# Half of a causal depthwise convolution moved from VectorE to GpSimd, inside a fused two-model forward pass

## The chip, the cores and the metric

The kernel is one program on one core of a Trainium2 chip. The core has five engines with an instruction queue each: TensorE (PE in the profile, its weight loads PEld), VectorE (DVE), ScalarE (ACT), GpSimd (POOL) and SyncE (SP, which here only issues transfers). They meet through semaphores alone. The metric is the device time of one execution, in microseconds, as the median of several runs.

## The reference

The program computes two models one behind the other on 256 tokens of width 1024: first a model of two layers (an "even" and an "odd" one), then a second of two layers with a feed-forward block, a mixer and another feed-forward block each. The change lies in the even layer of the first. Its left half is a gated convolution over time, 512 channels wide:

```
def _conformer_conv(u_val, u_gate, w_dw, b_dw, ln_g, ln_b):
    c = u_val.shape[-1]
    h = u_val * jax.nn.sigmoid(u_gate)
    h = jnp.pad(h, ((0, 0), (CONV_WIDTH - 1, 0), (0, 0)))
    y = lax.conv_general_dilated(h, w_dw[:, None, :].astype(h.dtype), (1,), 'VALID',
                                 dimension_numbers=('NWC', 'WIO', 'NWC'), feature_group_count=c)
    y = _layernorm(y + b_dw.astype(y.dtype), ln_g, ln_b)
    return jax.nn.silu(y)
```

The convolution is depthwise: each channel is the sum of 31 taps (CONV_WIDTH), a shifted copy of its own row times one weight. Its right half is causal attention with 8 heads of 64. Both halves are gated and go through one output projection, whose result is added to x.

## The kernel before

**Layout.** Activations lie channels on partitions, tokens along the row. The 512 channels of the convolution are four tiles of 128 channels by 256 tokens: `conv[:, c, :]`, with c from 0 to 3, and `hpad[:, c, :]`, the gated input with 30 zeros ahead of it. So tap k of tile c reads `hpad[:, c, k:k + 256]`, multiplies it by one weight per partition and adds it to `conv[:, c, :]`.

**The jobs.** The even layer projects its input in 14 jobs on TensorE (`job`, matmuls at line 697). Each takes two or four weight tiles in float32 as three passes of a high and a low part. ScalarE makes the high part of a weight tile (line 1346) and VectorE the low one (line 1727, `split_to`); the job waits for `tile_lo`. There is room for 6 split tiles (RING), so a tile's high part waits for the job that read its place last. ScalarE brings each job's result from PSUM.

**The convolution.** After job 3 VectorE multiplies value by gate into `hpad` (line 1808) and starts the four sums with tap 0 and the bias (line 1811). The other 30 taps are single instructions, a product and an addition in one (line 1818), put by hand in between: `taps(a, b)` is a loop over taps a to b - 1, four channel tiles each. Two taps (8 instructions) come behind the splits for each of jobs 4 to 12, which makes taps 1 to 18. Two more come in each of six hooks in the attention, taps 19 to 30.

**The attention.** It runs four pairs of heads in a pipeline of steps s = 0, 1, ... In one step VectorE takes the scores of pair s out of PSUM (line 1771), forms the negated maxima (lines 1774 and 1775), runs the hook, and scales the exponentials of pair s - 1 by their reciprocal sums (lines 1788, 1789, 1794; semaphore `p_made`). Three steps later it gates the pair's output (line 1839). ScalarE takes the exponentials (line 1395), TensorE turns them (line 797), ScalarE copies them out (line 1403), and TensorE multiplies by the values (line 772). Scores are made at line 760.

**What follows.** The output projection (line 811) takes the attention's half of the channels first. Ahead of its first matmul (`y_wait`, k == 4) TensorE waits for all taps and sums the four tiles of `conv` over the channels (line 838), which the layer norm needs. VectorE centres the tiles (line 1841), ScalarE squares them, TensorE sums the squares (line 843), and VectorE scales and gates (lines 1844 and 1846) while the projection of the attention's half runs.

**GpSimd** has four memsets and four transfers at the start (lines 640 to 650), and then three transfers that wait for far later layers (lines 658 and 660). It computes nothing else. `sg` is a scratch tile, unused in the even layer.

Of the kernel before, what the change touches and what calls it, by code (L numbers as in the profile page):

```python
# [17 lines left out]
ALU = mybir.AluOpType  # L18
# [6 lines left out]
T = 256  # L25
# [7 lines left out]
CONV = 31  # L33
# [325 lines left out]
def build(nc, x_in, stream, params, csts, bias_in, lora_in, final_g, vb2, sinks, out):  # L359
    ctx = ExitStack()  # L360
    with ctx:
        def sb(name, *shape):
            return ctx.enter_context(nc.sbuf_tensor(name, [P, *shape], F32))

        def flat(ap):
            return ap.rearrange("p a b -> p (a b)")
# [3 lines left out]
        def sem(name):  # L370
            if name not in names:
                names[name] = ctx.enter_context(nc.semaphore(name))
            return names[name]
# [9 lines left out]
        sg = sb("silu_gate", SS, T)  # L383
# [6 lines left out]
        def par(name, lo=0, n=None):  # L390
            o, w = PAR.at[name]
            return PARt[:, o + lo:o + (w if n is None else lo + n)]

        def cst(name, lo=0, n=None):
            o, w = CST.at[name]
            return CSTt[:, o + lo:o + (w if n is None else lo + n)]
# [20 lines left out]
        def at(*shape):  # L417

            n = int(np.prod(shape))
            o = place[0]  # L420
            place[0] = o + n
            assert o + n <= ARENA, o + n
            a = arena[:, o:o + n]
            if len(shape) == 1:
                return a
            letters = "abcdef"[:len(shape)]
            return a.rearrange(f"p ({' '.join(letters)}) -> p {' '.join(letters)}",
                               **{c: s for c, s in zip(letters, shape)})
# [38 lines left out]
        hpad = at(4, CONV - 1 + T + 2)  # L467
        ugate = at(4, T)
        conv = at(4, T)
# [163 lines left out]
        def arena_free(n):  # L633


            return n - 1 if n and PHASES[n - 1][0].startswith("ffn") else n

        @block.gpsimd
        def _(pool):
            pool.memset(hpad[:, :, 0:CONV - 1], 0.0)  # L640
            pool.memset(hidv.rearrange("p a b c d -> p (a b c d)"), 0.0)
            pool.memset(VCB.rearrange("p a b c -> p (a b c)"), 0.0)
            pool.memset(SC.rearrange("p a b c d -> p (a b c d)"), 0.0).then_inc(sem("zeros_made"), 1)

            pool.wait_ge(sem("x_loaded"), 16 * NTT)
            pool.wait_ge(sem(f"w_loaded{NS - 1}"), 16)
            pool.dma_start(CSTt[:, CST_HEAD:], csts[:, CST_HEAD:]).then_inc(sem("const_loaded"), 16)
            pool.dma_start(DIST.rearrange("p a b c -> p (a b c)"), bias_in).then_inc(sem("const_loaded"), 16)
            pool.dma_start(SINK, sinks.broadcast_to([P, NH])).then_inc(sem("const_loaded"), 16)
            pool.dma_start(VB2, vb2.broadcast_to([P, HD])).then_inc(sem("const_loaded"), 16)  # L650
            for l in range(2):

                n = [i for i, p in enumerate(PHASES) if p[:2] == ("mix", l)]
                if n:
                    pool.wait_ge(sem("const_loaded"), CONSTS)
                    if arena_free(n[0]):
                        pool.wait_ge(sem("x_made"), 4 * arena_free(n[0]))
                    pool.dma_start(lora[:], lora_in[l]).then_inc(sem("lora_loaded"), 16)
            pool.wait_ge(sem("x_made"), 4 * arena_free(len(PHASES)))
            pool.dma_start(FG, final_g.broadcast_to([P, D])).then_inc(sem("gain_loaded"), 16)  # L660
# [3 lines left out]
        def _(pe):  # L664
# [75 lines left out]
            def headnorm(kind, hn0, i, bank):  # L740

                width = HEADNORMS[kind][i][1]
                pe.wait_ge(sem("sq_made"), hn0 + i + 1)
                pe.matmul(PS[:, bank, 0:width], cst("blk"), sq[:, i, 0:width], start=True, stop=True)\
                  .then_inc(sem("ssq_made"), 1)
# [74 lines left out]
            def even_layer(tr0, jb0, hn0, n):  # L820
                for i in range(10):
                    job("even", tr0, jb0, i)
                for i in range(4):
                    headnorm("even", hn0, i, 4 + i)
                for i in range(10, 14):
                    job("even", tr0, jb0, i)
                pe.wait_ge(sem("job_out"), jb0 + 14)

                pe.wait_ge(sem("qk_made"), 4)
                attention("even", {"q": Q1}, {"k": lambda j, rows: K1[rows, j, :]}, lambda s: None)  # L830

                def y_wait(k):


                    if k == 4:
                        pe.wait_ge(sem("conv_step"), 4 * CONV)
                        for c in range(4):
                            ins = pe.matmul(PS[:, 4, 0:T], cst("ones"), conv[:, c, :], start=(c == 0), stop=(c == 3))
                        ins.then_inc(sem("ln_sum_made"), 1)
                    if k == 6:  # L840
                        pe.wait_ge(sem("convsq_made"), 1)
                        for c in range(4):
                            ins = pe.matmul(PS[:, 4, T:2 * T], cst("ones"), convsq[:, c, :],
                                            start=(c == 0), stop=(c == 3))
                        ins.then_inc(sem("ln_sum_made"), 1)
                    if k == 0:
                        pe.wait_ge(sem("y_conv_made"), 1)
                pe.wait_ge(sem("pair_out"), 4)
                out_projection("even", tr0, n, y_wait)
# [832 lines left out]
        def _(dve):  # L1682
            dve.wait_ge(sem("head_loaded"), HEAD)
            dve.wait_ge(sem("zeros_made"), 1)
            done = Steps(dve, "dve_step")
            for gain in ("b_q", "c_q", "d_q"):
                k = done(dve.tensor_scalar(par(gain), par(gain), HD ** -0.5, None, ALU.mult))
# [43 lines left out]
            def split_for(n):  # L1731

                split_to(SPLIT[now["kind"]][2][n])
# [70 lines left out]
            def even_layer(jb0, hn0):  # L1804
                for n in range(4):
                    split_for(n)
                dve.wait_ge(sem("job_out"), jb0 + 4)
                done.wait(done(dve.tensor_tensor(hpad[:, :, CONV - 1:CONV - 1 + T], conv, ugate, ALU.mult)))
                o = PAR.at["conv_w"][0]
                for c in range(4):  # L1810
                    dve.tensor_scalar(conv[:, c, :], hpad[:, c, 0:T], par("conv_w", c, 1), par("conv_b", c, 1),
                                      ALU.mult, ALU.add).then_inc(sem("conv_step"), 1)

                def taps(a, b):
                    with dve.Fori(a, b) as k:
                        for c in range(4):
                            dve.wait_ge(sem("conv_step"), k * 4 + (c - 3))
                            dve.scalar_tensor_tensor(conv[:, c, :], hpad[:, c, bass.ds(k, T)],  # L1818
                                                     PARt[:, bass.ds(k * 4 + (o + c), 1)], conv[:, c, :],
                                                     ALU.mult, ALU.add).then_inc(sem("conv_step"), 1)  # L1820

                for n in range(4, 14):
                    split_for(n)
                    for i in {11: [0], 12: [1], 13: [2, 3]}.get(n, []):
                        a, gain = ((Q1, "b_q"), (K1, "b_k"))[i // 2]
                        j = 2 * (i % 2)
                        scaled(hn0, i, [(flat(a[:, j:j + 2, :]), gain)])
                    if n < 13:  # L1830
                        taps(2 * n - 7, 2 * n - 5)

                def hook(s):
                    if s < 6:
                        taps(2 * s + 19, 2 * s + 21)

                dve.wait_ge(sem("job_out"), jb0 + 14)
                dve.wait_ge(sem("const_loaded"), CONSTS)
                attention("even", lambda c, pv: dve.tensor_tensor(YT[:, c.tile, :], pv, ZB[:, c.j, :], ALU.mult), hook)
                dve.wait_ge(sem("ln_sum_made"), 1)  # L1840
                dve.scalar_tensor_tensor(conv, rep(PS[:, 4, 0:T], 4), -1.0 / 512, conv, ALU.mult, ALU.add)\
                   .then_inc(sem("conv_centred"), 1)
                dve.wait_ge(sem("lnrs_made"), 1)
                dve.tensor_tensor(conv, conv, rep(lnrs, 4), ALU.mult).then_inc(sem("conv_scaled"), 1)
                dve.wait_ge(sem("conv_act"), 1)
                dve.tensor_tensor(YT[:, 0:4, :], conv, ZA, ALU.mult).then_inc(sem("y_conv_made"), 1)
# [345 lines left out]
```

## Time and profile before

| | |
|---|---|
| median of 3 runs | 1607.51 us |
| lowest and highest | 1598.91 and 1611.56 us |
| the profiled execution, its time | 1599.55 us |
| its span, first to last instruction | 1597.8 us |
| mean granted TensorE clock in it | 0.955 |
| busy: TensorE, VectorE, ScalarE, GpSimd | 91%, 54%, 43%, 0% |
| even layer, from the span's start | about 172 us |

All rows are from the one profiled execution. In a row of the timeline the first number is the start in us from the span's start, the second the us to the end of the group; then come engine, line, operation, the tile written and the tile read, shapes and count; idle time ahead of it stands in brackets with what ended it. The convolution's tiles lie in a large buffer which the profile calls `arena`. An instruction's duration includes its way in and out of the engine, and the next one starts a little before it ends: what a row of equal instructions costs is the distance from the first start to the next group's start.

### The profile page before, as it was taken

How to read it: one execution, taken by the hardware profiler on the slowest of the kernel's cores; microseconds unless marked ns; L12 is line 12 of the kernel's file. 1: busy time of each engine (PE TensorE's matmuls, PEld its weight loads, DVE VectorE, ACT ScalarE, POOL GpSimd, SP SyncE). 2: the span in 40 equal slices, each digit the busy share in tenths (PEclk: the TensorE clock that was granted, in tenths of full speed). 3: DMA queues.
4: the chain of work that ended last, by engine and by line, in shares of the span. 5: the costliest groups of instructions: out<-in, count | busy, mean ns of one | idle time of the engine just before them, and what ended most of it. 6: DMA issues, size and time to landing. Idle time of an engine off the chain costs nothing.

```text
span 1597.8 us, 28298 instructions
## 1 busy us (share of the span) xinstructions
PE 1455.9 (91%) x11842; PEld 1273.8 (80%) x11842; DVE 858.4 (54%) x1226; ACT 692.9 (43%) x1048; POOL 5.9 (0%) x15
## 2 busy tenths in 40 slices
PE   6977886888999989888899998999989988899998
PEld 6964676755899989767499998999989867489997
DVE  5876416744545557634454555545566644364554
ACT  5443336543444456421344444444445422254443
POOL 1000000000000000000000000000000000000000
PEclk9986998899999999979999998999999979999999
DMA  7421444115455444200455543555534200445552
GB/s 291 184 80 39 159 148 168 41 40 196 173 197 184 175 154 158 80 2 3 158 202 192 190 170 130 205 185 197 176 140 167 110 1 3 152 178 197 182 178 100
DMA packets 21741, 227.10 MB, mean 142 GB/s; under 512 B 2449, under 2 KB 2449, under 8 KB 3617
## 3 DMA queue, kind: packets, MB, share of 16 engines
q1 hardware_dynamic: 20880, 221.30, 37.9%
q0 software_dynamic: 784, 4.70, 0.9%
q8 instruction: 59, 0.97, 0.2%
q14 instruction: 18, 0.14, 0.0%
HBM read 224.94 MB, written 1.05 MB: 141 GB/s over the span
## 4 chain that ended last, share of the span: by engine, by line
PE 77%; DVE 11%; ACT 7%; DMA 3%; issue 2%; DVEq 0%; SPq 0%; ACTq 0%; PEldq 0%
PE PS L697 46%; PE PS L1005 14%; PE PS L811 6%; DMA weight_ring<-in_stream 2%; DVE w_lo L1945 2%; DVE w_lo L1727 1%; ACT arena L1323 1%; DVE arena L1703 1%; PE PS L1127 1%; PE PS L1185 1%; PE PS L1160 1%; ACT w_hi L1346 1%; PE PS L1191 1%; DVE arena L1818 1%; PE PS L1122 1%
## 5 line engine op out<-in xcount | busy, mean ns | idle before, releaser
L697 PE MATMUL PS<-hT_hi,w_hi 128*128 128x256 f32 x2136 | 615.1, 288 | 39.9 <-DVE hT_lo L1709 22.1
L697 PE MATMUL PS<-hT_lo,w_hi 128*128 128x256 f32 x2136 | 610.9, 286 | 0.0
L697 PE MATMUL PS<-hT_hi,w_lo 128*128 128x256 f32 x2136 | 610.9, 286 | 0.0
L697 PEld LDWEIGHTS PS<-hT_hi,w_hi 128*128 128x128 f32 x2136 | 416.6, 195 | 50.1 <-issue 46.1
L697 PEld LDWEIGHTS PS<-hT_lo,w_hi 128*128 128x128 f32 x2136 | 416.7, 195 | 3.8 <-issue 0.7
L697 PEld LDWEIGHTS PS<-hT_hi,w_lo 128*128 128x128 f32 x2136 | 416.4, 195 | 0.0
L1945 DVE TENSOR_TENSOR w_lo<-weight_ring,w_hi 128x1024 fp32r<-128x1024 f32 x176 | 207.2, 1219 | 17.7 <-ACT w_hi L1522 17.7
L1951 DVE TENSOR_TENSOR w_lo<-weight_ring,w_hi 128x1024 fp32r<-128x1024 f32 x88 | 107.8, 1225 | 156.6 <-ACT w_hi L1528 156.6
L1522 ACT ACTIVATE w_hi<-weight_ring 128x1024 fp32r<-128x1024 f32 x176 | 175.4, 1046 | 19.6 <-DMA weight_ring<-in_stream 19.6
L1727 DVE TENSOR_TENSOR w_lo<-weight_ring,w_hi 128x1024 fp32r<-128x1024 f32 x107 | 125.7, 1220 | 62.9 <-ACT w_hi L1346 62.7
L1528 ACT ACTIVATE w_hi<-weight_ring 128x1024 fp32r<-128x1024 f32 x88 | 93.1, 1058 | 104.4 <-PE PS L1005 104.4
L1005 PE MATMUL PS<-w_hi,act_hi 128*128 128x512 f32 x352 | 138.0, 392 | 0.0
L1005 PE MATMUL PS<-w_hi,act_lo 128*128 128x512 f32 x352 | 138.0, 392 | 0.0
L1005 PE MATMUL PS<-w_lo,act_hi 128*128 128x512 f32 x352 | 136.9, 389 | 0.0
L1548 ACT ACTIVATE silu_gate<-PS 128x256 f32<-128x256 f32 x88 | 33.7, 383 | 233.8 <-PE PS L697 233.8
L1346 ACT ACTIVATE w_hi<-weight_ring 128x1024 fp32r<-128x1024 f32 x107 | 106.5, 1050 | 28.4 <-DMA weight_ring<-in_stream 28.4
L1964 DVE TENSOR_TENSOR ffn_act<-silu_gate,PS 128x256 f32<-128x256 f32 x88 | 37.1, 421 | 144.5 <-ACT silu_gate L1548 144.5
L811 PE MATMUL PS<-weight_ring,yT 128*128 128x512 f32 x256 | 111.5, 594 | 0.6 <-issue 0.6
L811 PEld LDWEIGHTS PS<-weight_ring,yT 128*128 128x128 f32 x256 | 48.9, 191 | 61.4 <-issue 61.1
L1005 PEld LDWEIGHTS PS<-w_lo,act_hi 128*128 128x128 f32 x352 | 66.1, 188 | 14.4
L1005 PEld LDWEIGHTS PS<-w_hi,act_hi 128*128 128x128 f32 x352 | 66.4, 189 | 11.5
L1005 PEld LDWEIGHTS PS<-w_hi,act_lo 128*128 128x128 f32 x352 | 66.4, 189 | 10.6
(277 smaller groups left out, 1370.5 us busy)
## 6 DMA issues: line engine op xcount, KB each, us to landing
weight_ring<-in_stream SPq DMA_DIRECT2D x139, 1536.0 KB, 6.6
consts<-in_csts POOLq DMA_DIRECT2D x1, 1864.0 KB, 7.8
arena<-in_bias_in POOLq DMA_DIRECT2D x1, 1152.0 KB, 9.6
x_res<-in_x_in SPq DMA_DIRECT2D x2, 512.0 KB, 4.2
lora<-in_lora_in POOLq DMA_DIRECT2D x2, 512.0 KB, 5.4
x_out<-yT SPq DMA_DIRECT2D x2, 512.0 KB, 2.6
arena<-in_final_g POOLq DMA_DIRECT2D x1, 512.0 KB, 7.0
params<-in_params SPq DMA_DIRECT2D x1, 292.5 KB, 5.4
```

The costliest lines, as they stand in the source:

```text
L697: ins = pe.matmul(out, w[a], x[b], start=(start and i == 0), stop=(stop and i == 2))
L811: ins = pe.matmul(PS[:, 2 * t + half, :], YT[:, k, t * P:(t + 1) * P], w[:, half * 512:(half + 1) * 512], start=(i == 0), stop=(i == 7))
L1005: ins = pe.matmul(o, (Ah, Al)[x][:, s, t * P:(t + 1) * P], w[y][:, cols], start=(start and j == 0), stop=(stop and j == 2))
L1122: pe.matmul(o, Vret[:, c2, (2 * e + j) * P:(2 * e + j + 1) * P], STm[:, e, j, c2, :], start=True, stop=False)
L1346: act.activation(Wh[:, q % RING], Wr[:, tile % (3 * NS)], ACT.Copy).then_inc(sem("tile_hi"), 1)
L1522: act.activation(Wh[:, 3 * (i % SS) + part], Wr[:, 3 * (g % NS) + part], ACT.Copy)\
L1528: act.activation(Wh[:, 3 * (i % SS) + 2], Wr[:, 3 * ((tr0 + i) % NS) + 2], ACT.Copy)\
L1548: act.activation(sg[:, s, :], PS[:, 4 + s, 0:T], ACT.Silu).then_inc(sem("silu_made"), 1)
L1727: dve.tensor_tensor(Wl[:, q % RING], Wr[:, tile % (3 * NS)], Wh[:, q % RING], ALU.subtract)\
L1945: dve.tensor_tensor(Wl[:, u], Wr[:, 3 * ((tr0 + i) % NS) + part], Wh[:, u], ALU.subtract)\
L1951: dve.tensor_tensor(Wl[:, u], Wr[:, 3 * ((tr0 + i) % NS) + 2], Wh[:, u], ALU.subtract)\
L1964: dve.tensor_tensor(aT[:, s, :], sg[:, s, :], PS[:, 4 + s, T:2 * T], ALU.mult)\
```

## The change

Channel tiles 2 and 3 are computed on GpSimd. It waits for `conv_gated`, which VectorE now raises behind the gating product. Then, tap by tap, it does a product into the scratch tile `sg` and an addition into `conv`, each waiting for what it reads. VectorE keeps tiles 0 and 1, two instructions for a tap. It now takes three taps behind each of jobs 4 to 12 (taps 1 to 27, six instructions where eight stood) and one tap in each of the first three hooks (taps 28 to 30, two instructions where eight stood); hooks 3 to 5 are empty. TensorE's wait ahead of the channel sum becomes two: `conv_step` for VectorE's tiles and `conv_tap` for GpSimd's. VectorE waits for `conv_tap` as well ahead of the centring.

```
+            pool.wait_ge(sem("conv_gated"), 1)
+            for k in range(CONV):
+                for c in (2, 3):
+                    if k == 0:
+                        pool.tensor_scalar(conv[:, c, :], hpad[:, c, 0:T], par("conv_w", c, 1), par("conv_b", c, 1),
+                                           ALU.mult, ALU.add).then_inc(sem("conv_tap"), 1)
+                    else:
+                        pool.wait_ge(sem("conv_tap"), 2 * (k - 1) + (c - 2) + 1)
+                        pool.tensor_scalar(sg[:, c - 2, :], hpad[:, c, k:k + T], par("conv_w", 4 * k + c, 1), None,
+                                           ALU.mult).then_inc(sem("conv_part"), 1)
+                        pool.wait_ge(sem("conv_part"), 2 * (k - 1) + (c - 2) + 1)
+                        pool.tensor_tensor(conv[:, c, :], conv[:, c, :], sg[:, c - 2, :], ALU.add)\
+                            .then_inc(sem("conv_tap"), 1)
...
-                        pe.wait_ge(sem("conv_step"), 4 * CONV)
+                        pe.wait_ge(sem("conv_step"), 2 * CONV)
+                        pe.wait_ge(sem("conv_tap"), 2 * CONV)
...
-                done.wait(done(dve.tensor_tensor(hpad[:, :, CONV - 1:CONV - 1 + T], conv, ugate, ALU.mult)))
+                dve.tensor_tensor(hpad[:, :, CONV - 1:CONV - 1 + T], conv, ugate, ALU.mult).then_inc(sem("conv_gated"), 1)
+                dve.wait_ge(sem("conv_gated"), 1)
...
-                        for c in range(4):
-                            dve.wait_ge(sem("conv_step"), k * 4 + (c - 3))
+                        for c in range(2):
+                            dve.wait_ge(sem("conv_step"), k * 2 + (c - 1))
...
-                        taps(2 * n - 7, 2 * n - 5)
+                        taps(3 * n - 11, 3 * n - 8)
...
-                    if s < 6:
-                        taps(2 * s + 19, 2 * s + 21)
+                    if s < 3:
+                        taps(s + 28, s + 29)
...
+                dve.wait_ge(sem("conv_tap"), 2 * CONV)
```

## Rows read from the trace of the kernel before

**Rows 1.** The page: busy time by engine, and the chain's shares by line.

```profile
PE 1455.9 (91%) x11842; PEld 1273.8 (80%) x11842; DVE 858.4 (54%) x1226; ACT 692.9 (43%) x1048; POOL 5.9 (0%) x15
PE PS L697 46%; PE PS L1005 14%; PE PS L811 6%; DMA weight_ring<-in_stream 2%; DVE w_lo L1945 2%; DVE w_lo L1727 1%; ACT arena L1323 1%; DVE arena L1703 1%; PE PS L1127 1%; PE PS L1185 1%; PE PS L1160 1%; ACT w_hi L1346 1%; PE PS L1191 1%; DVE arena L1818 1%; PE PS L1122 1%
```

**Rows 2.** Busy time by stretch: jobs 4 to 13, attention, start of the output projection.

```profile
core 0: us, PE busy (x) PEld busy (x) DVE busy (x) ACT busy (x) POOL busy (x), PEclk, DMA share, GB/s
45.70:77.10 31.40, 31.40 (x263) 31.40 (x262) 30.61 (x59) 12.52 (x17) 0.00 (x0) 1.00 0.46 169
77.10:105.10 28.00, 26.68 (x200) 24.39 (x199) 18.96 (x34) 15.59 (x20) 0.00 (x0) 1.00 0.31 113
105.10:140.70 35.60, 17.36 (x89) 10.53 (x88) 33.33 (x81) 12.33 (x38) 0.00 (x0) 0.58 0.00 1
140.70:151.80 11.10, 11.06 (x25) 6.24 (x26) 1.23 (x1) 1.06 (x1) 0.00 (x0) 0.80 0.00 0
```

**Rows 3.** What TensorE waited for, 0 to 185 us: us, times, longest.

```profile
PE PS L797 <- DVE arena L1794: 9.1, 4, 3.9
...
PE PS L697 <- DVE w_lo L1727: 1.3, 1, 1.3
```

**Rows 4.** Timeline of VectorE: gating product, splits, and first taps.

```profile
43.20 1.23 DVE L1808 TENSOR_TENSOR arena<-arena 128x1024 f32<-128x1024 f32 x1 [2.33 <-ACT arena L1410]
...
45.77 2.35 DVE L1727 TENSOR_TENSOR w_lo<-weight_ring,w_hi 128x1024 fp32r<-128x1024 f32 x2
48.03 3.25 DVE L1818 SCALAR_TENSOR_TENSOR arena<-arena,params 128x256 f32<-128x256 f32 x8
```

**Rows 5.** Groups of VectorE, 45.7 to 105.2: busy us, mean ns, idle before.

```profile
L1818 DVE SCALAR_TENSOR_TENSOR arena<-arena,params 128x256 f32<-128x256 f32 x72 | 29.2, 478 | 0.0
L1727 DVE TENSOR_TENSOR w_lo<-weight_ring,w_hi 128x1024 fp32r<-128x1024 f32 x16 | 18.9, 1220 | 9.8 <-ACT w_hi L1346 9.8
L1758 DVE SCALAR_TENSOR_TENSOR arena<-arena,params 128x512 f32<-128x512 f32 x4 | 2.9, 744 | 0.0
```

**Rows 6.** Timeline of VectorE in the attention: parts of steps 2 to 5.

```profile
120.29 3.25 DVE L1818 SCALAR_TENSOR_TENSOR arena<-arena,params 128x256 f32<-128x256 f32 x8
123.45 0.16 DVE L1788 TENSOR_SCALAR arena<-arena 128x4 f32<-128x4 f32 x1
123.65 0.18 DVE L1789 RECIPROCAL arena<-arena 128x4 f32<-128x4 f32 x1
123.86 1.03 DVE L1794 TENSOR_TENSOR arena<-arena 128x256 f32<-128x256 f32 x2
124.81 0.95 DVE L1771 SCALAR_TENSOR_TENSOR arena<-arena,PS 128x768 f32<-128x768 f32 x1
...
130.29 1.03 DVE L1794 TENSOR_TENSOR arena<-arena 128x256 f32<-128x256 f32 x2
...
136.43 3.25 DVE L1818 SCALAR_TENSOR_TENSOR arena<-arena,params 128x256 f32<-128x256 f32 x8
```

**Rows 7.** The chain that ended last, end of the attention: start, us, what.

```profile
136.23 1.55 PE PS L797 x6
137.81 0.82 ACT lora L1403
138.67 1.57 PE PS L772 x8
140.26 0.43 DVE yT L1839
140.74 3.78 PE PS L838 x8
```

**Rows 8.** Timeline of GpSimd: two of its memsets.

```profile
0.74 0.20 POOL L640 MEMSET arena<- 128x120 f32 x1 [0.29 <-POOLq L2181]
0.88 0.53 POOL L641 MEMSET arena<- 128x512 f32 x1
1.34 0.53 POOL L642 MEMSET arena<- 128x512 f32 x1
```

More of the change, by code:

```diff
@@ L1815, in taps @@
                     with dve.Fori(a, b) as k:
-                        for c in range(4):
-                            dve.wait_ge(sem("conv_step"), k * 4 + (c - 3))
+                        for c in range(2):
+                            dve.wait_ge(sem("conv_step"), k * 2 + (c - 1))
                             dve.scalar_tensor_tensor(conv[:, c, :], hpad[:, c, bass.ds(k, T)],
```

## The prediction

> **What bounds the kernel now.** I read the page first: TensorE is busy 91% of the span, and the taps of line 1818 are 1% of the chain that ended last [rows 1]. So the change can only matter in the even layer's 172 us, and I read that layer stretch by stretch. In the jobs, from 45.7 to 105.1 us, TensorE hardly ever stands still and VectorE is busy too, 30.61 of the first 31.40 us [rows 2]; all the same TensorE waited for a split only once, 1.3 us [rows 3]. In the attention it is the other way round: VectorE is busy 33.33 of 35.60 us and TensorE 17.36 [rows 2], and TensorE's longest wait in all is for VectorE's scaling, 9.1 us [rows 3]. The attention is VectorE's stretch, and taps are a large part of it. It ends with a chain through TensorE, ScalarE and VectorE; at 140.74 TensorE begins the channel sum, which needs every tap [rows 7]. That is the point at which I measure both paths of the changed kernel.
>
> **What the change removes.** One tap on one tile costs VectorE 0.395 us: eight of them take from 120.29 to 123.45 [rows 6]. In the jobs 72 become 54 [rows 5], which frees 18 x 0.395 = 7.1 us. TensorE doesn't wait there, so this is worth nothing by itself, but it is slack, and I need it below. In the attention each of six hooks takes 3.16 us [rows 6]. Hook 5, at 136.43, runs beside the last chain [rows 6, 7] and is already free. Hooks 0 to 4 lie in VectorE's row: 5 x 3.16 = 15.8 us go, and 6 instructions of 0.395 stay in hooks 0 to 2, 2.4 us. That is 13.4 us gross. Not all of it is had. With the hooks gone the last two pairs run nose to tail on TensorE and ScalarE. From the end of pair 2's scaling, 130.29 + 1.03 = 131.3, to the end of the last gating product, 140.7, there are now 9.4 us. The work of two pairs in a row is 2 x (1.55 + 0.82 + 1.57) + 0.43 = 8.3 us [rows 7]. So the hook in this piece is worth 1.1 and not 3.2, and 2.1 us are given back. Net 11.3: without GpSimd's half the sum could begin at 140.7 - 11.3 = 129.4 us.
>
> **What it adds.** GpSimd waits for the gating product, which ends at 43.20 + 1.23 = 44.4 [rows 4]; its transfers are long issued. Then it does 2 first products and 60 pairs of a product and an addition, in order, the addition waiting for the product just before it. Nothing else is queued behind them but transfers for much later layers. TensorE's new wait is the costly one. The channel sum, the whole output projection, and behind them the residual and the next layer stand behind it in TensorE's queue. VectorE and ScalarE have nothing else to do by then, so each us by which GpSimd is late costs one us. Break even is at (140.7 - 44.4 - 0.6) / 60 = 1.59 us a pair; the whole gain is there below (129.4 - 45.0) / 60 = 1.41 us.
>
> No row shows a product or an addition on GpSimd. The nearest are its memsets. One of 512 columns costs 1.34 - 0.88 = 0.46 us, one of 120 costs 0.14 [rows 8], so about 0.25 us for 256 columns. That is one pass over a tile. Lower end: both instructions cost like memsets, 0.50 us a pair. Upper end: a product is two passes (a read, a write) and an addition three, none of them overlapped and each as dear as the 512-column memset, 5 x 0.46 = 2.3 us. I take five passes at the half of that, for half the columns: 5 x 0.23 = 1.15 us. To this come semaphores. On VectorE two tiny instructions that wait for each other start 0.20 us apart [rows 6]; one such wait in a pair, and a little for the other, is 0.25 us. So 1.40 us a pair if GpSimd is alone: it would end at 45.0 + 84 = 129, at the very moment when the attention does.
>
> The Trainium skill's page "GPSIMD Engine Reference", Performance versus the Vector engine, measures an addition of 2048 float32 columns at 4497 ns on GpSimd. An eighth of it is an estimate of 0.56 us for ours, beside 0.69 by my passes; by that the pair would be 1.27 us and the end 121. No row of before shows such an addition.
>
> It isn't alone. VectorE runs two-input instructions on the same memory nearly all the time: splits at (48.03 - 45.77) / 2 = 1.13 us [rows 4], 16 of them; 54 taps at 0.395; 4 instructions of line 1758 at about 0.67, their mean of 744 ns less the 0.08 by which a tap's 478 ns is over its 0.395 [rows 5]; in the attention 6 taps and 8 scalings at about 0.475 [rows 6]. This is 18.1 + 21.3 + 2.7 + 2.4 + 3.8 = 48.3 us, or 0.80 us for each pair of GpSimd. The disturbance to GpSimd lies between nothing and all of that: a pair costs 1.40 to 2.20 us. No row has the two engines at work together, so I take a little under the middle, 0.35 us, since GpSimd has the end of the attention, and the 9.8 us in which VectorE waits [rows 5], to itself. Then a pair is 1.75 us and GpSimd ends at 45.0 + 105 = 150.0. The channel sum begins at 150 in place of 140.7: **+9.3 us**. The attention at 129.4 is covered by it; its gain goes into a wait.
>
> **The clock.** The granted clock is 0.58 over the attention and 0.80 in the stretch behind it [rows 2]. The channel sum already starts at the lower level of 1.2 GHz after a thin stretch. So a longer wait changes nothing at this place, and I add nothing.
>
> **Sum.** The profiled execution took 1599.55 us (span 1597.8, and 1.75 around it); with +9.3 it is 1608.9. The median of the runs shown is 8.0 us above that execution, and I carry this over: 1607.5 + 9.3 = 1617.
>
> **Rivals.**
> 1. *GpSimd is in time.* A pair costs 1.41 us or less, also beside VectorE; the attention sets the end. For it: my price for GpSimd alone is just that, and much of the memset's price may be overlapped reading and writing. Against it: VectorE's two-input work. Result: 129.4 in place of 140.7, -11.3 us, 1596. Even this is only 0.7%.
> 2. *The two engines hold each other up, and the jobs starve* (the other side). If each two-input instruction of VectorE waits for one instruction of GpSimd, 1.15 / 2 = 0.575 us, the 74 of them in the jobs add 42.5 us and only 7.1 are slack, so the jobs end 35.4 us later. The 14 in the attention add 8. By then GpSimd is done or nearly so, and the channel sum starts at 129.4 + 35.4 + 8 = 173: +32 us, 1640. With x us for each instruction the sum moves by 74x - 7.1 + 14x - 11.3, which is over 16 us from x = 0.39. For it: VectorE is busy 30.61 of 31.40 us in the jobs [rows 2]. Against it: GpSimd's own gaps let VectorE through. The Trainium skill states this as a rule, in "SBUF — State Buffer", Who interferes with whom: a VectorE instruction with two SBUF inputs and a GpSimd one that reads SBUF share a read interface, the first to start holds it for its whole length, and the other is blocked. No row of before has both at work, so none agrees or disagrees yet.
> 3. *GpSimd's instructions are simply dear.* At the upper end of 2.3 us and 0.25 for semaphores a pair costs 2.55 us; the end is at 45 + 153 = 198, +57 us, 1665. For it: memsets are the simplest thing that the engine does. Against it: nothing that the profile shows.
>
> **Chances.** A measurement of this kernel tells about 1% from no change, 16 us. My forecast, GpSimd last with a pair at 1.6 to 1.85 us (0 to +16): 0.45. Rival 1 (down to -11, with run scatter perhaps -16): 0.20. Rival 2: 0.20, of which a third stays under +16. Rival 3, from +16 to +57: 0.15. Faster by over 1% is then 0.05, mostly scatter on rival 1; within 1% is 0.43 of the forecast, 0.15 of rival 1 and some of rival 2, rounded to 0.60; slower 0.35. The range goes from rival 1 with a little scatter, 1594, to well into rivals 2 and 3, 1650. The likeliest case alone is 1607 to 1624.
>
> **What would show it.** GpSimd's rows: pair after pair from 44.5 us, spaced 1.75 us, and closer together while VectorE waits around 80 us and from 130 us on. VectorE's taps in the jobs start-to-start at about 0.4 us, and jobs that end near 105: right for me; 0.6 us and more, with TensorE waiting for line 1727, is rival 2. The last gating product (line 1839) near 130. Ahead of TensorE's channel sum an idle time of 20 us that GpSimd ended: if it is missing, rival 1; if it is 60 us, rival 3. I am wrong in kind if anything outside the even layer moves.

## The result

The changed kernel takes 1630.11 us, the median of 4 runs from 1628.53 to 1631.39. The kernel before takes 1604.97 us (4 runs, 1598.91 to 1611.56). The ratio is 1.0159, with a 95% interval of 1.0125 to 1.0193: slower by 1.6%, about 25 us. I had forecast 1617 us and no difference that can be told from none. The change cost nearly three times the 9.3 us of my sum.

The profiled execution took 1631.39 us with a span of 1629.6, against 1599.55 and 1597.8: 31.8 us of span. That is more than the 25.1 us between the medians, because the profiled execution of the kernel before lies 5.4 us under its median and that of the changed kernel 1.3 over. The page of the changed kernel shows GpSimd in the chain that ended last, with 4% and 3% of the span for its two lines; in the kernel before it wasn't there at all [rows 1].

```profile
PE 1457.4 (89%) x11842; PEld 1274.5 (78%) x11842; DVE 852.7 (52%) x1164; ACT 692.8 (43%) x1048; POOL 125.6 (8%) x137
PE 73%; DVE 9%; POOL 7%; ACT 6%; DMA 3%; issue 2%; SPq 0%; DVEq 0%; ACTq 0%; PEldq 0%
PE PS L710 41%; PE PS L1019 14%; PE PS L824 6%; POOL silu_gate L659 4%; POOL arena L662 3%; DMA weight_ring<-in_stream 2%; DVE w_lo L1961 2%; DVE w_lo L1741 1%; ACT arena L1337 1%; DVE arena L1717 1%; PE PS L1141 1%; PE PS L1199 1%; PE PS L1205 1%; PE PS L1136 1%; ACT w_hi L1360 1%
```

Two queries place the loss. First, what TensorE waited for in the first 215 us (us, times, longest); then its timeline at that wait. Line 852 is the channel sum, line 662 GpSimd's addition.

```profile
PE PS L852 <- POOL arena L662: 33.6, 1, 33.6
...
PE PS L710 <- DVE w_lo L1741: 3.1, 2, 1.8
```

```profile
134.84 1.55 PE L785 MATMUL PS<-lora,arena 128*64 128x256 f32 x8 [0.90 <-ACT lora L1417]
169.98 3.55 PE L852 MATMUL PS<-arena,consts 128*128 128x256 f32 x8 [33.60 <-POOL arena L662]
```

The attention is over, TensorE does its last product with the values at 134.84, and then it stands still for 33.6 us until GpSimd's last addition. The channel sum starts at 169.98 in place of 140.74 [rows 7], 29.2 us later. At the first addition of the layer's output to x the two kernels are at 200.19 and 171.56 us, 28.6 apart, and at the same place of the odd layer 28.1. The other 3.7 us of the 31.8 come up in the later layers, which do the same in both. The four executions of the kernel before lie 12.7 us apart, so I read nothing into them.

The stretches of [rows 2] in the changed kernel, in the same columns: GpSimd is busy throughout, VectorE has 25.13 us of work in the third where it had 33.33, and in the fourth nothing but GpSimd moves.

```profile
45.70:77.10 31.40, 30.12 (x252) 29.94 (x251) 31.40 (x41) 12.56 (x18) 30.48 (x25) 1.00 0.46 166
...
105.10:140.70 35.60, 21.43 (x123) 14.55 (x122) 25.13 (x46) 12.34 (x38) 34.01 (x39) 0.64 0.00 0
140.70:151.80 11.10, 0.00 (x0) 0.00 (x0) 0.00 (x0) 0.00 (x0) 10.60 (x14) 0.50 0.00 0
```

GpSimd's own groups over the whole span: count, busy us, mean ns of one, idle before.

```profile
L659 POOL TENSOR_SCALAR silu_gate<-arena,params 128x256 f32<-128x256 f32 x60 | 71.2, 1187 | 0.0
L662 POOL TENSOR_TENSOR arena<-arena,silu_gate 128x256 f32<-128x256 f32 x60 | 46.3, 771 | 5.0
L655 POOL TENSOR_SCALAR arena<-arena,params 128x256 f32<-128x256 f32 x2 | 3.4, 1680 | 27.5 <-DVE arena L1822 27.5
```

Its timeline shows two prices for the same pair. Beside VectorE's splits a product takes up to 2.95 us. With VectorE quiet, a pair takes (168.11 - 132.27) / 21 = 1.71 us: product to addition 1.00, addition to product 0.70.

```profile
45.23 3.35 POOL L655 TENSOR_SCALAR arena<-arena,params 128x256 f32<-128x256 f32 x2 [27.47 <-DVE arena L1822]
48.57 1.08 POOL L659 TENSOR_SCALAR silu_gate<-arena,params 128x256 f32<-128x256 f32 x1
...
97.01 2.94 POOL L659 TENSOR_SCALAR silu_gate<-arena,params 128x256 f32<-128x256 f32 x1
100.04 1.00 POOL L662 TENSOR_TENSOR arena<-arena,silu_gate 128x256 f32<-128x256 f32 x1
...
132.27 0.92 POOL L659 TENSOR_SCALAR silu_gate<-arena,params 128x256 f32<-128x256 f32 x1
133.28 0.72 POOL L662 TENSOR_TENSOR arena<-arena,silu_gate 128x256 f32<-128x256 f32 x1
133.98 0.92 POOL L659 TENSOR_SCALAR silu_gate<-arena,params 128x256 f32<-128x256 f32 x1
...
168.11 0.92 POOL L659 TENSOR_SCALAR silu_gate<-arena,params 128x256 f32<-128x256 f32 x1
```

And VectorE pays as well. These are its groups from 45.7 to 105.2 us, answering to [rows 5], and a stretch of its timeline, where six taps go from 54.51 to 58.23: 0.62 us each, where eight took 3.16 [rows 6]. A split's mean is 1387 ns where it was 1220.

```profile
L1833 DVE SCALAR_TENSOR_TENSOR arena<-arena,params 128x256 f32<-128x256 f32 x49 | 31.3, 703 | 0.0
L1741 DVE TENSOR_TENSOR w_lo<-weight_ring,w_hi 128x1024 fp32r<-128x1024 f32 x16 | 21.5, 1387 | 6.1 <-ACT w_hi L1360 6.1
```

```profile
54.51 3.80 DVE L1833 SCALAR_TENSOR_TENSOR arena<-arena,params 128x256 f32<-128x256 f32 x6
58.23 2.55 DVE L1741 TENSOR_TENSOR w_lo<-weight_ring,w_hi 128x1024 fp32r<-128x1024 f32 x2
```

A quarter fewer taps thus took more time. In this window 49 of the 54 keep VectorE busy for 31.3 us, where all 72 took 29.2, and the last matmul of the jobs starts at 109.01 us instead of 104.82. That loss of 4.2 us lies under GpSimd's late end and isn't seen in the time. It becomes visible as soon as GpSimd is made faster, as the first experiment shows.

### The profile page after: what moved, and what is told of

The parts are those of the page before. It is cut to its first block, busy times and chain, and to the rows that moved or that the text cites. A ratio compares the mean times of both kernels' runs of the same rounds, so it can differ in the third digit from the quotient of the medians.

```text
span 1629.6 us, 28256 instructions
## 1 busy us (share of the span) xinstructions
PE 1457.4 (89%) x11842; PEld 1274.5 (78%) x11842; DVE 852.7 (52%) x1164; ACT 692.8 (43%) x1048; POOL 125.6 (8%) x137
## 3 DMA queue, kind: packets, MB, share of 16 engines
HBM read 224.94 MB, written 1.05 MB: 139 GB/s over the span
## 4 chain that ended last, share of the span: by engine, by line
PE 73%; DVE 9%; POOL 7%; ACT 6%; DMA 3%; issue 2%; SPq 0%; DVEq 0%; ACTq 0%; PEldq 0%
PE PS L710 41%; PE PS L1019 14%; PE PS L824 6%; POOL silu_gate L659 4%; POOL arena L662 3%; DMA weight_ring<-in_stream 2%; DVE w_lo L1961 2%; DVE w_lo L1741 1%; ACT arena L1337 1%; DVE arena L1717 1%; PE PS L1141 1%; PE PS L1199 1%; PE PS L1205 1%; PE PS L1136 1%; ACT w_hi L1360 1%
```

## The experiments

My theory after the result: GpSimd's chain is last by its own price, 1.71 us a pair and not 1.40, and it and VectorE hold each other up. The rival: the price is ordinary, and the mutual blocking makes both dear. The 1.71 us in the stretch where VectorE is quiet already speak against it as a whole. Beside these stands the question whether the loss in the jobs is real when GpSimd is not last.

Edits are shown against the changed kernel, except in the last two experiments: the first of these starts from the kernel before, the second from the first. A ratio is to the kernel before, measured again each time: 1606.58 us for the first experiment and for the taps placed otherwise, 1602.35 us for the one tile and for GpSimd in the attention only. A time without a ratio is of a single execution, good for its trace and not for a difference of a few us.

**The product as a tensor_tensor.**

```
-                        pool.tensor_scalar(sg[:, c - 2, :], hpad[:, c, k:k + T], par("conv_w", 4 * k + c, 1), None,
-                                           ALU.mult).then_inc(sem("conv_part"), 1)
+                        pool.tensor_tensor(sg[:, c - 2, :], hpad[:, c, k:k + T],
+                                           par("conv_w", 4 * k + c, 1).broadcast_to([P, T]), ALU.mult)\
+                            .then_inc(sem("conv_part"), 1)
```

> The changed kernel, but each product on GpSimd is a tensor_tensor with the weight broadcast along the row, in place of a tensor_scalar that takes the weight as a scalar operand. In the changed kernel the product costs 1.00 us from start to start and the addition 0.70 us, once VectorE is quiet. Theory A (the dear thing is the tensor_scalar with its scalar operand): the product falls to 0.8 us or less, a pair to about 1.5 us, the channel sum starts about 12 us earlier than 169.9 us, the kernel takes 1618 us. Theory B (any multiplying instruction costs that, or reading hpad does): the product stays at 1.00 us and the kernel at 1630 us. If two tensor inputs were what costs, as my passes had it, it would become slower.

Measured: 1614.82 us, ratio to before 1.0058 (1.0033 to 1.0082). Theory A holds for the price; the channel sum starts at 154.75 us, 15.2 earlier than in the changed kernel. With VectorE quiet the product now takes 0.69 us from start to start, like the addition, and a pair 1.37 us:

```profile
151.14 0.72 POOL L663 TENSOR_TENSOR arena<-arena,silu_gate 128x256 f32<-128x256 f32 x1
151.82 0.61 POOL L659 TENSOR_TENSOR silu_gate<-arena,params 128x256 f32<-128x256 f32 x1
152.51 0.72 POOL L663 TENSOR_TENSOR arena<-arena,silu_gate 128x256 f32<-128x256 f32 x1
```

The product went from 1.00 to 0.69 us although it now reads a second tensor. So it was the form of the instruction that was dear, not the passes over memory. But look at VectorE in the same run, and at TensorE's waits:

```profile
55.06 5.00 DVE L1834 SCALAR_TENSOR_TENSOR arena<-arena,params 128x256 f32<-128x256 f32 x6
59.97 3.32 DVE L1742 TENSOR_TENSOR w_lo<-weight_ring,w_hi 128x1024 fp32r<-128x1024 f32 x2
```

```profile
PE PS L711 <- DVE w_lo L1742: 8.1, 2, 6.3
PE PS L774 <- DVE arena L1773: 7.9, 1, 7.9
PE PS L811 <- DVE arena L1809: 5.5, 3, 3.1
...
PE PS L853 <- POOL arena L663: 5.0, 1, 5.0
```

Six taps take 4.91 us, 0.82 each, over twice the 0.395 of before. GpSimd's instructions start 0.76 to 0.88 us apart at this place, so the two engines take turns, one tap to one instruction. TensorE waits 8.1 us for splits, and 7.9 ahead of the attention's first scores, which wait for line 1773: these start at 121.56 us, where they started at 105.79 before the change and at 110.47 in the changed kernel. The attention ends at 150 us, almost 10 later than before the change, and GpSimd still ends 5 us behind it. So the faster GpSimd delays VectorE more: of the 33.6 us that TensorE waited for it, 15.2 are gained, and only 5 are left because the attention itself now ends 13 us later. This is the mechanism of my rival 2.

**GpSimd only writes.**

```
-            for k in range(CONV):
...
+            for k in range(180):
+                if k:
+                    pool.wait_ge(sem("conv_tap"), k)
+                pool.memset(sg[:, :, :].rearrange("p a b -> p (a b)"), 0.0).then_inc(sem("conv_tap"), 1)
```

> Leaves out the two channel tiles of GpSimd: it writes zeros to the scratch tile 180 times instead, each waiting for the one before, and reads nothing. VectorE's work is that of the changed kernel. If what slows VectorE's taps from 0.395 to about 0.63 us and its splits is GpSimd's reading, taps go back to 0.395 us, the jobs end near 105 us and the attention near 129.4 us. If any work of GpSimd on the memory slows VectorE, taps stay at 0.5 us or more and the jobs end near 109. GpSimd's writes end at 45 + 180 x 0.5 to 0.6 = 135 to 153 us, so the attention's end must be read in the trace and the time is set by those writes: 1595 to 1615 us.

Measured: 1607.21 us, a single execution. VectorE's two-input instructions go as if GpSimd weren't there, though that engine is busy 28.3 of the 31.4 us from 45.7 us on. Groups from 45.7 to 105.2:

```profile
L1825 DVE SCALAR_TENSOR_TENSOR arena<-arena,params 128x256 f32<-128x256 f32 x54 | 22.9, 481 | 0.2 <-DVE arena L1825 0.2
L1733 DVE TENSOR_TENSOR w_lo<-weight_ring,w_hi 128x1024 fp32r<-128x1024 f32 x16 | 18.9, 1220 | 14.5 <-ACT w_hi L1352 14.5
```

The means are 481 and 1220 ns, against 478 and 1220 in [rows 5], and VectorE waits 14.5 us for ScalarE where it waited 9.8. The last matmul of the jobs starts at 104.29 us. So GpSimd's writing costs the taps and splits nothing; what holds them up goes away with its reading. (The run leaves out the arithmetic together with the reads and doesn't part the two.)

One form is held up even by writes: VectorE's tensor_scalar, which has one tensor as input. The small one on 4 columns (line 1788 before, 1794 here) lasts 163 ns in the mean before and 407 here, up to 560. The reciprocal just behind it stays at 178 ns. The two first products of VectorE's tiles, also tensor_scalars, take 1.23 us here, where four took 1.30 before. In the changed kernel the small one lasts 377 ns in the mean.

The run also shows the floor of the attention: its last gating product (line 1846) starts at 126.73.

```profile
122.15 0.56 DVE L1794 TENSOR_SCALAR arena<-arena 128x4 f32<-128x4 f32 x1 [0.74 <-ACT arena L1401]
...
126.73 0.42 DVE L1846 TENSOR_TENSOR yT<-PS,arena 128x256 f32<-128x256 f32 x1 [2.08 <-PE PS L777]
```

It ends at 127.2 us, where the prediction had 129.4 for an undisturbed VectorE. The Trainium skill states this in "SBUF — State Buffer", Who interferes with whom: a VectorE instruction with two SBUF inputs shares a read interface with a GpSimd one that reads SBUF, and doesn't meet one that only writes. By that rule the traces agree, 0.62 and 0.82 us a tap beside reads and 0.41 beside writes.

**VectorE without its taps.**

```
-                        pe.wait_ge(sem("conv_step"), 2 * CONV)
+                        pe.wait_ge(sem("conv_step"), 2)
...
-                        taps(3 * n - 11, 3 * n - 8)
...
-                        taps(s + 28, s + 29)
```

> Leaves out taps 1 to 30 of VectorE's two channel tiles; GpSimd's work is that of the changed kernel. In the changed kernel its 60 pairs took 121.3 us, 2.02 a pair, and 1.71 once VectorE was quiet. If the 0.31 us between is VectorE's two-input instructions holding it up, and more of that is taps than splits, a pair falls to about 1.80 us, GpSimd ends near 49 + 108 = 157 us and the kernel takes about 1617 us. If GpSimd runs at 2.02 whatever VectorE does, it ends at 170 and the time stays at 1630. The jobs end at 105 to 106 us.

Measured: 1624.16 us, a single execution. GpSimd's pairs run from 48.57 to 166.8 us, 1.97 us each, where they took 2.02. I had expected 1.80. The taps thus cost GpSimd only 0.05 us a pair; of the 0.31 between a quiet and a mean pair nearly all is left when they are gone. The trace shows what does it. Both engines at one place, VectorE's splits first:

```profile
56.85 2.70 DVE L1741 TENSOR_TENSOR w_lo<-weight_ring,w_hi 128x1024 fp32r<-128x1024 f32 x2 [2.86 <-ACT w_hi L1360]
```

And GpSimd, at the pair of splits before that (from 51.09 us) and at this one:

```profile
51.30 1.61 POOL L662 TENSOR_TENSOR arena<-arena,silu_gate 128x256 f32<-128x256 f32 x1
52.89 1.89 POOL L659 TENSOR_SCALAR silu_gate<-arena,params 128x256 f32<-128x256 f32 x1
...
57.31 2.94 POOL L659 TENSOR_SCALAR silu_gate<-arena,params 128x256 f32<-128x256 f32 x1
60.34 0.75 POOL L662 TENSOR_TENSOR arena<-arena,silu_gate 128x256 f32<-128x256 f32 x1
```

The product at 57.31, which starts 0.5 us behind the first of two splits, is held for both, 2.94 us instead of 0.92. It isn't always so: at the pair before, an addition and a product share the hold, 1.61 and 1.89 us. In the changed kernel too there are both cases: 2.95 us for the product at 52.34, and 2.16 for the one at 58.00, which starts 0.2 us ahead of the splits, with 1.14 for the addition behind it. I read this as a hold-up by the length of what stands in front: GpSimd suffers from the long splits, and VectorE's short taps suffer from GpSimd.

**The product with a constant.**

```
-                        pool.tensor_scalar(sg[:, c - 2, :], hpad[:, c, k:k + T], par("conv_w", 4 * k + c, 1), None,
+                        pool.tensor_scalar(sg[:, c - 2, :], hpad[:, c, k:k + T], 0.5, None,
```

> The changed kernel with each product of GpSimd multiplied by the constant 0.5 and not by the weight, so the convolution's weights of two tiles are left out from tap 1 on. It tells what makes the tensor_scalar cost 1.00 us where the tensor_tensor costs 0.69. If it is the fetching of the scalar from memory, the product falls to about 0.7 us and GpSimd ends near 150 us. If it is the form of the operation itself, the product stays at 1.00 us and GpSimd ends at 170 us.

Measured: 1619.76 us, a single execution, with the channel sum at 161.46 us. Neither answer came out whole. A quiet product lasts 0.85 us and takes 0.93 from start to start, between 0.69 and 1.00:

```profile
145.05 0.85 POOL L659 TENSOR_SCALAR silu_gate<-arena 128x256 f32<-128x256 f32 x1
145.98 0.72 POOL L662 TENSOR_TENSOR arena<-arena,silu_gate 128x256 f32<-128x256 f32 x1
146.67 0.85 POOL L659 TENSOR_SCALAR silu_gate<-arena 128x256 f32<-128x256 f32 x1
```

The scalar from memory is 0.07 us of the extra 0.31, the tensor_scalar form itself 0.24. Why the form costs that, no run here tells. GpSimd ends 8.5 us earlier than in the changed kernel, where 60 x 0.07 = 4.2 explain one half. The other half isn't explained; it may lie in how the instructions happen to meet the splits.

**Products first.**

```
+                for c in (2, 3):
+                    if k:
                         pool.wait_ge(sem("conv_part"), 2 * (k - 1) + (c - 2) + 1)
```

> The changed kernel with the order on GpSimd changed: for each tap both products, then both additions, so that no instruction waits for the one just before it except the second product after an addition has ended. In the changed kernel GpSimd's idle time ahead of the additions is 5.0 us in all, 0.08 each. If that wait is all that the semaphores cost, a quiet pair falls from 1.71 to 1.63 us at most and the channel sum starts up to 5 us earlier. If the wait also hides in the durations, it falls further, towards 1.5. If one instruction must be over before the next starts anyway, nothing changes.

Measured: 1627.14 us, a single execution; the channel sum starts at 163.99 us, 6 earlier. A tap of both tiles, quiet, takes 147.99 - 144.82 = 3.17 us, 1.585 a pair against 1.71:

```profile
144.82 1.82 POOL L659 TENSOR_SCALAR silu_gate<-arena,params 128x256 f32<-128x256 f32 x2
146.61 1.40 POOL L664 TENSOR_TENSOR arena<-arena,silu_gate 128x256 f32<-128x256 f32 x2
147.99 1.82 POOL L659 TENSOR_SCALAR silu_gate<-arena,params 128x256 f32<-128x256 f32 x2
```

A wait for the instruction just before costs 0.12 us a pair, the 0.08 of idle time and a little overlap. My prediction had 0.25 for it. Only part of the 6 us is this gain, though: GpSimd also started 1.05 us earlier in this execution, and its first two products, which here began before the splits, took 1.2 us and not 3.3. From there a pair takes (163.9 - 45.4) / 60 = 1.97 us in the mean, 0.05 less than in the changed kernel.

**One tile instead of two.** Tile 3 goes to GpSimd, tiles 0 to 2 stay.

```
-                for c in range(2):
+                for c in range(3):
...
-                        taps(3 * n - 11, 3 * n - 8)
+                        taps(2 * n - 7, 2 * n - 5)
...
-                    if s < 3:
-                        taps(s + 28, s + 29)
+                    if s < 6:
+                        taps(2 * s + 19, 2 * s + 21)
```

> Only channel tile 3 goes to GpSimd, in the changed kernel's form; VectorE keeps three tiles, two taps of each behind jobs 4 to 12 (6 instructions, as in the changed kernel) and two of each in six hooks (6 instructions, 8 in the kernel before). GpSimd has 30 pairs at 2.02 us and ends near 109 us, long before it is needed. Theory A (the only harm of the change is GpSimd's late end): the jobs end at 105 us, hooks 0 to 4 save 5 x 0.79 = 4 us, the channel sum starts at 136 to 137 us, the kernel is 4 us faster than before. Theory B (two-input instructions of VectorE wait for GpSimd's wherever the two meet): the jobs end 4 us later, as in the changed kernel, where the last matmul started at 109.0 and not 104.8 us, and the sum starts at 140 to 141 us: no gain at all.

Measured: 1603.72 us, ratio 0.9992 (0.9958 to 1.0025). GpSimd is done at 115 us, long before it is wanted, and still nothing is won. The groups of VectorE from 45.7 to 105.2:

```profile
L1832 DVE SCALAR_TENSOR_TENSOR arena<-arena,params 128x256 f32<-128x256 f32 x47 | 30.1, 706 | 0.0
L1740 DVE TENSOR_TENSOR w_lo<-weight_ring,w_hi 128x1024 fp32r<-128x1024 f32 x16 | 22.5, 1447 | 7.3 <-ACT w_hi L1359 7.3
```

The jobs' last matmul starts at 111.13 us (104.82 before) and the channel sum at 143.56 (140.74). So the jobs lost 6.3 us and the attention won back 3.5. That is theory B, and 2 us worse than it had said: in this place the hold-up, not the end of GpSimd alone, makes the offload worthless.

**The kernel before, taps placed otherwise.**

```
-                        taps(2 * n - 7, 2 * n - 5)
+                        t = {n: 1 + 2 * (n - 4) for n in range(4, 10)}
+                        t.update({10: 18, 11: 20, 12: 22, 13: 24})
+                        taps(t[n], t[n + 1])
...
-                    if s < 6:
-                        taps(2 * s + 19, 2 * s + 21)
+                    at_ = (24, 24, 25, 26, 27, 29, 31)
+                    if s < 6 and at_[s] < at_[s + 1]:
+                        taps(at_[s], at_[s + 1])
```

> The kernel before, all taps on VectorE, only placed otherwise: five more taps behind job 9, where VectorE waits 8.7 us for ScalarE, and five fewer in hooks 0 to 3. If VectorE's row sets the attention, as the prediction had it, and the wait behind job 9 is slack, the channel sum starts 5 x 1.58 = 7.9 us earlier, less what TensorE and ScalarE take back: 133 to 135 us in place of 140.7, and the kernel is 6 to 8 us faster, 0.4 to 0.5%. If the attention is bound by the chain through TensorE and ScalarE, nothing changes.

Measured: 1595.53 us, ratio 0.9931 (0.9905 to 0.9957), and the channel sum starts at 132.52 us. That is 8.2 us earlier than before, against 5 x 1.58 = 7.9 in the plan. The 28 instructions behind job 9, with the 8 of job 8 ahead of them, fill the time in which VectorE waited for ScalarE:

```profile
69.57 14.33 DVE L1818 SCALAR_TENSOR_TENSOR arena<-arena,params 128x256 f32<-128x256 f32 x36
84.71 4.63 DVE L1727 TENSOR_TENSOR w_lo<-weight_ring,w_hi 128x1024 fp32r<-128x1024 f32 x4 [0.81 <-ACT w_hi L1346]
```

This confirms the reading that the attention was VectorE's stretch and that the jobs had slack. It is faster than both kernels and moves nothing to another engine.

**GpSimd in the attention only**, on top of the rebalanced kernel: taps 24 to 30 of tiles 2 and 3, with the product as a tensor_tensor.

```
+            for k in range(24, CONV):
+                for c in (2, 3):
...
-                    at_ = (24, 24, 25, 26, 27, 29, 31)
+                    for k in {1: (24,), 2: (25,), 3: (26,), 4: (27, 28), 5: (29, 30)}.get(s, ()):
+                        for c in range(2):
```

> The rebalanced kernel with GpSimd in the attention only: taps 24 to 30 of tiles 2 and 3, 14 pairs with the product as a tensor_tensor (1.37 us each when alone), VectorE the same taps of tiles 0 and 1. 20 taps on VectorE's row in hooks 0 to 3 become 6, up to 5.5 us, and the floor is the chain that the run with writes only showed, 127 us. Collisions are with 14 two-input instructions only, up to 0.4 us each. I expect the channel sum at 129 to 131 us against 132.5 in the rebalanced kernel, 1 to 3 us faster than that: 0.991 to 0.993 of before. If the collisions eat the gain it is equal to the rebalanced kernel, and if GpSimd's pairs come late (it waits for VectorE's tap 23) the sum waits for GpSimd.

Measured: 1593.3 us, ratio 0.9925 (0.9896 to 0.9954), the same as the rebalanced kernel within the intervals of the ratios; the channel sum starts at 134.15 us, even 1.6 later than there, where I had expected 129 to 131. VectorE's part of step 2 shows why:

```profile
116.12 1.35 DVE L1854 SCALAR_TENSOR_TENSOR arena<-arena,params 128x256 f32<-128x256 f32 x2
117.39 0.57 DVE L1803 TENSOR_SCALAR arena<-arena 128x4 f32<-128x4 f32 x1
118.00 0.18 DVE L1804 RECIPROCAL arena<-arena 128x4 f32<-128x4 f32 x1
118.21 1.84 DVE L1809 TENSOR_TENSOR arena<-arena 128x256 f32<-128x256 f32 x2
119.97 0.94 DVE L1786 SCALAR_TENSOR_TENSOR arena<-arena,PS 128x768 f32<-128x768 f32 x1
```

Two taps, the small tensor_scalar, the reciprocal and two scalings take 119.97 - 116.12 = 3.85 us, where the rebalanced kernel needs 2.94 for them and two taps more (115.23 to 118.17). The scalings last 1.84 us together instead of 1.03. The small tensor_scalar on 4 columns takes 0.57 instead of 0.16; it is the form that GpSimd's writes alone held up too. Line 1786, with one input from PSUM, keeps its 0.94 us, and so do the reductions.

## Why the prediction was wrong, point by point

**What bounded the kernel.** Right. The attention was VectorE's row and the jobs had slack; the rebalanced kernel shows both at once.

**The gain in the attention.** Nearly right: 129.4 us predicted for an undisturbed VectorE, 127.2 in the run with writes only. The step that was off is the 2.1 us that I gave back. I had laid the last two pairs nose to tail, 8.3 us from the end of pair 2's scaling to the last gating product; in that run it is 6.1 us (121.07 to 127.15), so the two overlap, and nearly all of the gross 13.4 us is there. In the changed kernel the last gating product ended at 136.85, 9.7 us later than with writes only. The first scores account for 5.2 of it (110.47 against 105.26 us). In the attention the held scalings, taps and small tensor_scalars show about 3 us more; the rest isn't traced.

**The wait at the channel sum.** Right in kind: GpSimd is last, and each us of it costs one. 20 us of idle time were named, 33.6 came.

**The price of a pair, the step that failed.** My sum rested on 1.40 us for a pair alone and 1.75 beside VectorE. Alone it is 1.71, which is over the break-even of 1.59 even without any disturbance. Beside VectorE I had 1.75 us; it is (169.84 - 48.57) / 60 = 2.02. Its parts:

| term | predicted | measured |
|---|---|---|
| start | 44.4 | 45.23 |
| first two products | 0.6 us | 3.3 us |
| product, by my passes | 0.46 us | 0.92 us |
| addition | 0.69 us | 0.70 from start to start |
| waits in a pair | 0.25 us | 0.08 us idle |
| disturbance by VectorE | 0.35 us | 0.31 |
| pair in all | 1.75 us | 2.02 us |

The addition was right. The disturbance came out right too, but I had taken it from between nothing and 0.80 us, so that is luck in good part. It comes mostly from the splits and hardly from the taps: 0.26 of the 0.31 us are left in the run without VectorE's taps. The waits were too dear by 0.17 us, which hides part of the error. The mis-sized term is the product, 0.92 us where I had 0.46. I priced it by passes over memory, two against the addition's three, from memsets that have no arithmetic. On this engine the tensor_scalar form costs more than the tensor_tensor, 1.00 against 0.69 us from start to start. Sixty times (2.02 - 1.75) is 16.2 us. The first two products, 3.3 us in place of 0.6 and begun 0.8 late, make 3.6. Together 19.8: the end at 169.8 and not at 150.0.

**Rival 1** fell: with the cheaper product a quiet pair does cost 1.37 us, under the 1.41 that I had asked for, and the kernel is still slower than before, since beside VectorE the pair takes 1.79, (154.7 - 47.6) / 60. **Rival 3** met the product (2 x 0.46 = 0.92 us) by coincidence, since the tensor_tensor with one more input is cheaper, and it made the addition twice as dear as it is.

**Rival 2** was right as a mechanism and far too large: the jobs ended 4.2 us later and not 35. I charged 0.575 us for each of 74 instructions. The measured delay is 0.62 - 0.395 = 0.23 us for a tap and 1.39 - 1.22 = 0.17 for a split. With 54 taps and 16 splits that is 15 us, and besides the 7.1 us of slack VectorE's waiting for ScalarE shrank from 9.8 to 6.1 us, which leaves 4.3. With the cheap product the delay of a tap rises to 0.43 us, the jobs end 8.5 late and the attention's first scores start 15.8 late, nearer to the rival but still under half of its 35. A hold for the whole length of the instruction in front would cost more than these delays: a tap and an instruction of GpSimd, 0.395 and 0.69 us alone, take 0.82 us together and not 1.08. My sum charged VectorE nothing for GpSimd; in the changed kernel GpSimd's late end covered this error. I think the dear product spared VectorE because it reads for a smaller share of its time; that is argued, no run isolates it.

**The clock.** Right: the channel sum took 3.55 us after 33.6 us of idle time and 3.78 before [rows 7], and the granted clock was 0.50 over its first 2.5 us in both, the lower level of 1.2 GHz. From the start of the sum to the first addition to x it is 30.8 us before and 30.2 after, so the longer wait cost nothing behind it. The busy time of the first 2.5 us after the change, columns as in [rows 2]:

```profile
169.98:172.50 2.52, 2.52 (x6) 2.07 (x7) 0.00 (x0) 0.00 (x0) 0.00 (x0) 0.50 0.00 0
```

**The chances.** I held the forecast itself for likeliest and put 0.35 on slower by over 1%. Having taken one value between bounds of 0.75 and 2.55 us, with 60 in a row and no cover at the end, I should have seen that each 0.1 us of error is 6 us. The break-even of 1.59 us lay in the middle of those bounds before any disturbance, and the disturbance, up to 0.80, goes one way only.

## What to carry to other kernels

A second engine that reads the same memory is no free engine beside a VectorE that is busy with two-input instructions: count how many of those stand opposite it, and charge each with a wait before the offload's gain is booked. Price an offloaded chain by its break-even per instruction pair, and look how much of the bound lies above. Look first for idle time of the engine that has the work already: five taps moved into an 8.7 us wait brought 8.2 us, and moving 62 instructions of VectorE away cost 25 us.

## What the runs showed of the hardware that I had not expected

- On GpSimd a product by tensor_scalar with a weight from memory takes 1.00 us for 128 x 256 float32, with a constant 0.93, and as a tensor_tensor with the weight broadcast along the row 0.69, like the addition at 0.69 to 0.70.
- A GpSimd product that starts behind the first of two splits of VectorE can be held for both, 2.94 us for 0.92. In other places two instructions of GpSimd share the hold, 1.61 and 1.89 us.
- One tap and one instruction of GpSimd in turn take 0.82 us together, where alone they take 0.395 and 0.69, 1.08 in all. So neither keeps the other out for the whole of its own time.
- GpSimd's memsets, back to back, don't slow VectorE's two-input instructions: 481 ns against 478. But they slow VectorE's tensor_scalar on 4 columns, 407 ns against 163. Beside GpSimd's products and additions the taps take 703 and, in the cheaper form, 884 ns.
- "GPSIMD Engine Reference" of the Trainium skill, Performance versus the Vector engine, gives 4497 ns for an addition of 2048 columns; the estimate for 256 was 0.56 us, the trace has 0.72 with 0.70 from start to start.
